# A two-layer trunk in float32 halves: the low halves of the projection weights move from GpSimd to VectorE

## What is computed

```python
def trunk_layer(x, cond, lp_norm, lp_mix, lp_moe, ctx, lam_init):
    mod = jax.nn.silu(cond) @ w_mod_l + b_mod_l
    sh1, sc1, g1, sh2, sc2, g2 = jnp.split(mod[..., None, :], 6, axis=-1)
    h = rmsnorm(x, norm_mix_l) * (1.0 + sc1) + sh1
    y, new = mixer_sublayer(h, lp_mix, ctx, lam_init)   # h @ w_in, then mixers A, B, C, D
    x = x + g1 * y
    h = rmsnorm(x, norm_ffn_l) * (1.0 + sc2) + sh2
    x = x + g2 * hier_moe(h, *lp_moe)
...
    branches = jnp.stack([ya, yb, yc, yd], axis=2)
    proj = jnp.einsum('btnw,nwd->btnd', branches, w_branch)
    gates = jax.nn.sigmoid(gt.reshape(B, T, N_BRANCH, D_MODEL))
    out = jnp.sum(gates * proj, axis=2) @ w_out
```

## Time and profile before

| | |
|---|---|
| time, median of 3 runs | 1972.37 us (1972.34 to 1978.46) |
| profiled execution | 1976.06 us, of which span 1974.3 us |
| PE busy | 1692.2 us, 86% of the span |
| DVE busy | 1028.7 us, 52% |
| ACT busy | 874.8 us, 44% |
| POOL busy | 651.3 us, 33% |

### The profile page before, as it was taken

One profiled execution on the slowest core, in us unless ns is written; L12 is line 12 of the kernel. 1 busy time (PEld: TensorE's weight loads), 2 busy tenths in 40 slices (PEclk: granted clock), 3 DMA queues, 4 the chain that ended last, 5 costly groups with the idle time before them and its releaser, 6 DMA issues. The chain is left out here.

```text
span 1974.3 us, 30300 instructions
## 1 busy us (share of the span) xinstructions
PE 1692.2 (86%) x9725; PEld 1350.9 (68%) x9725; DVE 1028.7 (52%) x1795; ACT 874.8 (44%) x1493; POOL 651.3 (33%) x407
## 2 busy tenths in 40 slices
PE   3799998997999848999839999989989998399994
PEld 2588786775777636777627887767767786377773
DVE  0315447663451246899632263585634513399885
ACT  0343343443443326777513333444435333177773
POOL 1454452332466610000014454533234774000001
PEclk9999998998999968999959999999989998699997
DMA  7522332423364238999872232432435441599994
GB/s 261 213 97 75 110 123 81 133 104 117 149 214 157 89 124 289 363 372 355 299 275 89 86 96 89 134 116 78 155 118 193 150 145 58 187 353 368 349 371 181
DMA packets 117321, 361.10 MB, mean 183 GB/s; under 512 B 11772, under 2 KB 31804, under 8 KB 117184
## 3 DMA queue, kind: packets, MB, share of 16 engines
q1 hardware_dynamic: 112864, 343.63, 48.8%
q0 software_dynamic: 4320, 15.76, 2.1%
HBM read 338.57 MB, written 20.77 MB: 182 GB/s over the span
## 5 line engine op out<-in xcount | busy, mean ns | idle before, releaser
L716 POOL TENSOR_TENSOR wlo<-raw,whi 128x1024 fp32r<-128x1024 f32 x204 | 492.8, 2421 | 632.7 <-ACT whi L851 632.7
L1106 PE MATMUL G<-whi,hhi 128*128 128x512 f32 (+1 forms) x1440 | 582.3, 404 | 20.2 <-ACT pB L918 8.9
L1108 PE MATMUL G<-whi,hlo 128*128 128x512 f32 (+1 forms) x1440 | 563.5, 391 | 0.0
L1107 PE MATMUL G<-wlo,hhi 128*128 128x512 f32 (+1 forms) x1440 | 563.3, 391 | 0.0
L1498 DVE TENSOR_TENSOR wlo<-raw,whi 128x1024 fp32r<-128x1024 f32 x288 | 343.8, 1222 | 65.5 <-ACT whi L1029 62.8
L1029 ACT ACTIVATE whi<-raw 128x1024 fp32r<-128x1024 f32 x288 | 304.2, 1060 | 103.5 <-DMA raw<-in_units 38.4
L1106 PEld LDWEIGHTS G<-whi,hhi 128*128 128x128 f32 x1440 | 275.1, 191 | 96.7 <-DVE wlo L1498 15.9
L1108 PEld LDWEIGHTS G<-whi,hlo 128*128 128x128 f32 x1440 | 274.5, 191 | 59.1
L1107 PEld LDWEIGHTS G<-wlo,hhi 128*128 128x128 f32 x1440 | 275.3, 191 | 49.7
L851 ACT ACTIVATE whi<-raw 128x1024 fp32r<-128x1024 f32 x204 | 213.7, 1055 | 203.5 <-PE G L1108 135.1
L1126 PE MATMUL O<-raw,cond 128*32 128x128 f32 x1280 | 52.4, 332 | 63.4 <-DMA raw<-in_units 46.5
(11 more groups left out here) (293 smaller groups left out, 2229.4 us busy)
## 6 DMA issues: line engine op xcount, KB each, us to landing
raw<-in_units SPq DMA_DIRECT2D x588, 512.0 KB, 5.0
hs<-h_sorted SPq DMA_DIRECT2D x12, 514.0 KB, 7.6
y_sorted<-yo POOLq DMA_DIRECT2D x12, 512.0 KB, 7.5
bias<-in_nat_bias SPq DMA_DIRECT2D x16, 256.0 KB, 3.0
pC<-g_scratch SPq DMA_DIRECT2D x8, 512.0 KB, 9.4
h_sorted<-sig POOLq DMA_DIRECT2D x6, 514.0 KB, 13.3
x_scratch<-pA SPq DMA_DIRECT2D x2, 1536.0 KB, 13.2
pA<-x_scratch SPq DMA_DIRECT2D x2, 1536.0 KB, 8.1
```

Source lines behind the costliest of these rows:

```text
L716: lo_done.of(nc.gpsimd.tensor_tensor(wlo[:, k, :], raw[:, POS_OF[g] % RAW, :], whi[:, k, :].bitcast(F32), ALU.subtract))
L1106: nc.tensor.matmul(dst, st_hi, mv_hi, start=start, stop=False)
L1107: nc.tensor.matmul(dst, st_hi, mv_lo, start=False, stop=False)
L1108: return nc.tensor.matmul(dst, st_lo, mv_hi, start=False, stop=stop)
```

## The change

`split` leaves POOL's program and enters DVE's, with the same operands and the same signal. The two calls in `norm 0` now follow DVE's two scalings of x; the call for g + 2 is now the first thing that DVE does at product g, ahead of a branch's eviction and of the steps after g. ACT, PE and SP run the same code.

```diff
-                def split(g):
-                    pool.wait_ge(*hi_done.at(l, g))
-                    k = g % CONV
-                    lo_done.of(nc.gpsimd.tensor_tensor(wlo[:, k, :], raw[:, POS_OF[g] % RAW, :], whi[:, k, :].bitcast(F32),
-                                                       ALU.subtract))
-
...
-                        if s[1] == 0:
-                            split(0)
-                            split(1)
...
-                        if g + 2 < NG:
-                            split(g + 2)
...
+                def split(g):
+                    dve.wait_ge(*hi_done.at(l, g))
+                    k = g % CONV
+                    lo_done.of(tt(wlo[:, k, :], raw[:, POS_OF[g] % RAW, :], whi[:, k, :].bitcast(F32), ALU.subtract))
+
...
+                        if w == 0:
+                            split(0)
+                            split(1)
...
+                        if g + 2 < NG:
+                            split(g + 2)
```

## The result

| | before | after |
|---|---|---|
| median | 1973.63 us (1968.52 to 1980.31, 20 runs) | 1986.81 us (1978.65 to 1992.40, 20 runs) |
| profiled execution's span | 1974.3 us | 1984.7 us |
| DVE busy | 1028.7 us | 1149.5 us |
| POOL busy | 651.3 us | 171.0 us |

What follows compares the result with a forecast made beforehand. PE was taken to bound the projections, apart from a few waits. Per layer -2.7 - 7.1 + 0 + 15 + 6 = +11.2 us, +22.4 for two layers, gave 1995 us, 1.1% slower, range 1974 to 2014.

Steps and rivals of the forecast that it cites:

- Norm 0: Start of the layer: DVE's two scalings end earlier without POOL's low halves; -2.7 us per layer.
- Bq: Bq's eviction before product 26: `kdup` shrinks, PE's wait and the slower clock behind it go; -7.1 us per layer.
- B's attention: Attention of B: DVE's wait for `whi` plus low half replaces POOL's lock, 2.2 against 2.1 us per unit; 0.
- C's attention: Attention of C: DVE's cycle grows from 5.77 to 8.0 us, above PE's 6.82; +15 us per layer.
- product 58: C's attention: PE waits for branch (0, 1)'s eviction, which begins only after the low half; about 3 us.
- the two `mod`: C's attention: PE waits for DVE at `mod` 55, about 4 us, and at `mod` 59, about 5 us.
- D and `hr 1`: Attention of D and after: DVE's cycle stays within PE's, single waits are left; +6 us per layer.
- `gt 0`: Attention of D: its copy on ACT comes later, moving the next load, `whi` and PE's `mod`; 2.3 us.
- the eviction and the short units: Attention of D: the eviction at 69, 0.7 us, and the short units after 73 and 74, 1.8 us.
- The freed port wins: Rival: PE's slack of one product absorbs DVE's longer cycle in C and D, gains stay; 1953 us, chance 0.08.
- DVE waits for loads too: Rival: `whi` behind loads after a `mod` delays DVE at more places; +9 us per layer, 2013 us, chance 0.13.
- It evens out: Rival: C's lag is absorbed in part, D's by half; 1968 to 1977 us, chance 0.14.

Runs made afterwards that it cites:

- h54: Against the kernel before: DVE makes the low halves of units 0 to 53 of each layer, POOL those from 54 on; 1942.13 us, ratio 0.9843.
- aftersn: Against the changed kernel: the low half of g + 2 stands behind the first scaling of product g instead of ahead of it; 1950.29 us.
- wait_only: Against the changed kernel: low halves of units 54 to 81 make only 64 of 1024 columns, order kept; 1949.01 us.
- pool_again: Against the changed kernel: at products 20 to 27 POOL also makes an unused subtraction of 1024 columns on other buffers; 2005.87 us.
- lag1: Against the changed kernel: at product g DVE makes the low half of g + 1 instead of g + 2; 1982.90 us.

## Why the prediction was right, and where it wasn't

- **Norm 0**, -2.7: measured -2.3 and -4.4. The mechanism as told. The layers differ mostly by the first product, which ran 0.5 us longer than before in layer 0 and 1.1 us shorter in layer 1; I have not traced that further.
- **Bq**, -7.1: -7.0 and -5.8. Both terms, the wait and the clock behind it, were right: 4.2 and 2.9 us. (I took 4.4 us for the product at full clock; it is 4.18. And the scalings of the earlier trace rows end 0.2 us behind POOL's low half, not exactly with it.) In layer 1 the clock's part was 1.6 us.
- **B's attention**, 0: -5.4 and -3.2. This is the step that failed. I set the lock on the scalings against the low half's place in the chain, unit by unit, and there it holds: from product 47 to 55 neither kernel gains on the other. But I read what POOL locks only in the units, and wrote of `hr 0` and D's ropes that they "lose" something or "fall into a wait" without pricing it. PE's waits in this stretch stand behind them. Timeline of the kernel before, at `hr 0`:

```profile
286.76 2.40 POOL L716 TENSOR_TENSOR wlo<-raw,whi 128x1024 fp32r<-128x1024 f32 x1 [2.53 <-ACT whi L851]
...
289.70 2.27 POOL L722 TENSOR_TENSOR st<-st,cval 128x12 f32<-128x12 f32 x1
...
292.28 2.85 DVE L1498 TENSOR_TENSOR pA<-pA,st 128x512 f32<-128x512 f32 x1 [10.63 <-POOL st L787]
...
296.38 2.88 DVE L1498 TENSOR_TENSOR pA<-pA,st 128x512 f32<-128x512 f32 x1
...
302.44 0.95 DVE L1498 TENSOR_TENSOR prob<-S,bias 128x768 f32<-128x768 f32 x1
...
307.40 0.76 PE L1106 MATMUL G<-whi,hhi 128*128 128x512 f32 x1 [2.24 <-ACT pA L918]
```

  And DVE's first step of B's first unit in the kernel after:

```profile
287.58 0.96 DVE L1487 TENSOR_TENSOR prob<-S,bias 128x768 f32<-128x768 f32 x1 [2.36 <-PE S L1322]
```

  In the kernel before, two operations of 0.69 us take 2.85 and 2.88, and B's first unit starts at 302.44; with the 12.1 us gained up to there added, the kernel after starts it at 299.7, when PE's scores are there. So it is 2.8 us late, its exponentials hold ACT, ACT's eviction of the last product comes late, and PE waits 2.24 us. Three engines lie between lock and wait, and I had stopped at the first. The lock, 4.35 us in the two operations, isn't the only cause: `hr 0` also began 4.4 us later than after the change, since POOL's reciprocal roots stood behind POOL's own low half at 286.76. By these times either of the two alone would have fitted into DVE's slack; no run separates them. After the change this wait is gone; two small ones, 1.56 and 1.03 us, stand a unit later. At D's rope (kernel before, then after):

```profile
327.47 3.50 DVE L1498 TENSOR_TENSOR pB<-pA,rope_t 128x512 f32<-128x512 f32 x3
```

```profile
313.23 1.35 DVE L1487 TENSOR_TENSOR pB<-pA,rope_t 128x512 f32<-128x512 f32 x3
...
318.10 0.55 PE L1373 MATMUL T<-ident,pA 128*128 128x128 f32 x3 [2.39 <-DVE probT L1735]
```

  PE's wait for it fell from 3.94 to 2.39 us. In layer 0 another 2.0 us are the product behind the old wait. The stretch was mis-sized by 4.3 us per layer on average, 8.6 in all, which is as much as the prediction's whole excess. That this stretch's gain comes from `hr 0` and the rope is read from the traces; `h54` shows only that it comes with the units up to 53.
- **C's attention**, +15: +13.5 and +14.4. The cycle was 7.8 us where I said 8.0, the stretch 70.1 us where I said 69.4 (the terms that I gave, 64, 2 and 3, make 69). That the sum came out is in part luck, since its terms were off and cancelled: product 58 cost 1.1 us, counted from the start of product 56, and not 3, because PE has 2.5 us of attention steps between products 57 and 58, behind which most of the eviction hides; and the two `mod` cost 5.2 and 6.1, not 4 and 5, because PE's clock fell during the waits; from product 60 to 67 it was 1.2 us, where I had 2.1. I had charged the clock in the gain at Bq and not in the loss here.
- **D and `hr 1`**, +6: +7.1 and +6.9. The wait at product 80 was to be 2.2 us and is 1.95; `gt 0`, 2.3, was 3.0, of which 1.3 is again the clock of the `mod`; the eviction and the short units, 2.5 together, were 3.0. These are layer 0's.
- **Rivals.** *The freed port wins* needed the lag of one product to absorb an 8 us cycle: it did up to product 55, then PE waited. *DVE waits for loads too*: the wait after `mod` at 55 is there (ACT 2.88 us, DVE 5.41 with the exponentials), as charged, and no others came out on PE. *It evens out* needed half to two thirds of C's loss to be absorbed; 13.5 and 14.4 us of 15 were there.

## What to carry to other kernels

A move that changes the time little may be a gain and a loss of several times the size, in different stretches: take the start of each stage in both traces and subtract, and keep the engine for the stretches where it wins. For work that one engine hands to another in order, the place can matter more than the engine: here the same 1.2 us cost 20 us per layer behind a wait for its operand and nothing where its operand was one step old. When a lock is suspected, follow every operation that it lengthens to the bound engine, through as many engines as it takes, and look at what else stands in a queue behind the work that you move.

## What was not expected of the hardware

- A wait of PE of 4.6 us costs 6.3: the granted clock behind it was 0.50, and 64 small matmuls took 3.64 us instead of 1.96. Behind the 2.16 us wait of `aftersn` at the same place they took 3.44 us, behind that of 1.85 us in `wait_only`, at the next `mod`, 1.95. The length of the wait alone doesn't decide: in the kernel before, the `mod` after product 67 stood behind a wait of 3.28 us and took 1.95. So a wait may cost its length or up to 1.7 us more here; a forecast should carry both.
- The lock works both ways: POOL's multiplication of 512 columns took 1.87 us in `pool_again`, beside DVE's low halves. In `lag1` it took 1.04, and there it was DVE's three rope operations that took 1.74 us instead of 0.55.
